# Order of VectorE's instructions in the down projection of a retention, attention and FFN block

## The reference

```python
h = rmsnorm(x, mix_norm_g); z = h @ w_in
x = x + concat([retention(...), mla(...)]) @ w_o
h = rmsnorm(x, ffn_norm_g)
x = x + (silu(h @ w_ffn_gate) * (h @ w_ffn_up)) @ w_ffn_down     # D_FF = 2816
gate = sigmoid(rmsnorm(x, ple_norm_g) @ w_ple_gate)
x = x + gate * (p @ w_ple_proj)
return rmsnorm(x, final_norm_g)
```

## Time and profile before

| what | us |
|---|---|
| median of 3 runs | 1279.24 |
| the profiled execution | 1279.47 |
| its span | 1277.7 |
| busy TensorE (matmul) | 1245.1 |
| busy VectorE | 730.6 |
| busy ScalarE | 480.3 |
| busy GpSimd | 495.1 |

### The profile page before, as it was taken

How to read it: one execution, slowest core, us unless ns; L and a number is a source line. 1 busy time by engine, 2 the same in 40 slices (tenths; PEclk the granted TensorE clock), 3 DMA queues, 4 the chain that set the end, 5 groups by cost and what they waited for, 6 DMA issues and landing times.

```text
span 1277.7 us, 16752 instructions
## 1 busy us (share of the span) xinstructions
PE 1245.1 (97%) x6008; PEld 1046.6 (82%) x6008; DVE 730.6 (57%) x1194; ACT 480.3 (38%) x875; POOL 495.1 (39%) x510
## 2 busy tenths in 40 slices
PE   9999999989998999999999999999999999999997
PEld 8888888877888888878888888888888878788886
DVE  4734444476566226854445454444489999964433
ACT  6622222246565114533333333333344343414421
POOL 2534444440000002364335554334399887610001
PEclk9999999989999999999999999999999999999999
DMA  9411111010012400144233323223454545330002
GB/s 344 147 38 34 50 34 33 1 42 1 0 66 73 143 1 1 38 120 124 85 85 119 120 87 124 93 81 115 156 184 161 191 169 178 115 116 1 1 34 99
DMA packets 101932, 115.10 MB, mean 90 GB/s; under 512 B 4832, under 2 KB 67680, under 8 KB 101856
## 3 DMA queue, kind: packets, MB, share of 16 engines
q1 hardware_dynamic: 101424, 113.57, 27.2%
q10 hardware_dynamic: 432, 0.54, 0.1%
HBM read 90.49 MB, written 23.59 MB: 89 GB/s over the span
## 4 chain that ended last, share of the span: by engine, by line
PE 85%; issue 5%; DVE 4%; POOL 2%; DMA 2%; ACT 2%; SPq 0%; POOLq 0%; ACTq 0%; DVEq 0%
PE PS L1644 10%; PE PS L1642 10%; PE PS L1643 10%; PE PS L206 6%; PE PS L208 6%; PE PS L207 6%; PE PS L1976 4%; PE PS L1977 4%; PE PS L1978 4%; PE PS L994 3%; PE PS L1010 3%; PE PS L2328 2%; PE PS L2330 2%; PE PS L2329 2%; PE PS L789 2%
## 5 line engine op out<-in xcount | busy, mean ns | idle before, releaser
L206 PE MATMUL PS<-WF,HTH 128*128 128x512 f32 (+1 forms) x448 | 177.1, 395 | 1.6 <-DVE WF L184 0.9
L208 PE MATMUL PS<-WF,HTL 128*128 128x512 f32 (+1 forms) x448 | 173.9, 388 | 0.0
L207 PE MATMUL PS<-WF,HTH 128*128 128x512 f32 (+1 forms) x448 | 173.7, 388 | 0.0
L1363 DVE TENSOR_TENSOR X<-X,PS 128x512 f32<-128x512 f32 x172 | 109.9, 677 | 67.4 <-PE PS L208 52.6
L1642 PE MATMUL PS<-HTH,WF 128*128 128x512 f32 x336 | 131.0, 390 | 0.0
L1643 PE MATMUL PS<-HTL,WF 128*128 128x512 f32 x336 | 130.8, 389 | 0.0
L1644 PE MATMUL PS<-HTH,WF 128*128 128x512 f32 x336 | 130.7, 389 | 0.0
L1575 DVE TENSOR_TENSOR WF<-RAW,WF 128x512 fp32r<-128x512 f32 x63 | 69.6, 1106 | 82.4 <-ACT WF L1565 82.4
L1642 PE MATMUL PS<-WF 128*128 128x512 f32 x252 | 98.6, 391 | 2.9 <-issue 2.9
L206 PEld LDWEIGHTS PS<-WF,HTH 128*128 128x128 f32 x448 | 84.7, 189 | 17.5 <-DVE WF L184 1.3
L1644 PE MATMUL PS<-WF 128*128 128x512 f32 x252 | 98.7, 392 | 0.0
(11 more groups left out here) (254 smaller groups left out, 2804.2 us busy)
## 6 DMA issues: line engine op xcount, KB each, us to landing
hid<-TMP SPq DMA_DIRECT2D x74, 256.0 KB, 2.3
TMP<-hid SPq DMA_DIRECT2D x25, 512.0 KB, 5.0
RAW<-in_w_ffn_gate SPq DMA_DIRECT2D x22, 512.0 KB, 4.2
RAW<-in_w_ffn_up SPq DMA_DIRECT2D x22, 512.0 KB, 5.4
RAW<-in_w_ffn_down SPq DMA_DIRECT2D x22, 512.0 KB, 4.1
X<-in_x SPq DMA_DIRECT2D x16, 512.0 KB, 5.3
RAW<-in_w_in SPq DMA_DIRECT2D x32, 256.0 KB, 3.9
TAB<-hid SPq DMA_DIRECT2D x9, 512.0 KB, 4.7
```

The lines of the kernel that those rows point to most:

```text
L206: nc.tensor.matmul(dst, HTH[:, k, tok], w_h, start=(k == 0), stop=False)
L207: nc.tensor.matmul(dst, HTH[:, k, tok], w_l, start=False, stop=False)
L208: last = nc.tensor.matmul(dst, HTL[:, k, tok], w_h, start=False, stop=(k == K - 1))
L1363: nc.vector.tensor_tensor(x, x, src, ALU.add).then_inc(done, 1)
```

## The change

In each step of Down, VectorE's split of a moving operand is issued ahead of all four additions to X instead of between the second and the third. This holds for `ring_lo` (steps 0 to 31) and for the `down_lo` of steps 32 and 33. Pieces, the two last `down_lo` and the streams of all other engines are unchanged.

```diff
             for s in range(STEPS):
-                add_step(e, s, 0)
-                add_step(e, s, 1)
                 if s + 3 < STEPS:
                     ring_lo(e, s + 3)
                 elif s < STEPS - 1:
                     down_lo(e, LAST_ORDER[s + 3 - STEPS])
+                add_step(e, s, 0)
+                add_step(e, s, 1)
                 add_step(e, s, 2)
                 add_step(e, s, 3)
                 if s >= 18 and s % 4 == 2 and s <= 30:
                     piece_lo(e, (s - 10) // 4)
```

## The result

The changed kernel takes 1290.3 us in the median of 6 runs (1287.15 to 1292.87), the kernel before 1278.36 (6 runs, 1275.46 to 1279.64). The ratio is 1.0095, 95% interval 1.0077 to 1.0114: slower by about 12 us. The forecast was 1288.7.

The account below looks back on a forecast made before the run. It took Down to be bound by VectorE and GpSimd, nearly full and taking turns. 1279.24 us plus 2.3 + 5.0 + 4.0 - 4.8 + 3.0 = +9.5 gave 1288.7, own range 1286.5 to 1291, wider 1284.5 to 1291.5.

Parts of the forecast that it names:

- What bounds the stage: In Down, VectorE and GpSimd are nearly full and take turns, each waiting for the other's whole instruction; 4.8 us of waiting.
- Step 2, 2.3 us: TensorE starts step 2 of Down 2.3 us later, waiting for an addition behind a split; bounds 0 to 2.5.
- put off to steps 6 to 9: If no wait came at step 2 of Down, the same 2.3 us would come at steps 6, 7 or 9.
- Step 20, 5.0 us: Step 20 of Down waits 5.0 us for an addition behind a piece (two L184 instructions) and a split; 3.1 to 5.4.
- Step 28, 4.0 us: Step 28 of Down waits 4.0 us for an addition behind a piece and a split; 3.1 to 5.4.
- The 4.8 that go: The 4.8 us of waits in Down before the change are replaced by the new ones: -4.8.
- The clock, 3.0 us: TensorE's clock falls in Down behind the waits at steps 20 (1.3) and 28 (1.7), not step 2: +3.0, bounds 0 to 5.
- The sum: Waits and clock in Down add up to +9.5 us, so the median becomes 1288.7.
- VectorE's busy time: VectorE's busy time in Down, 189.0 of 196 us before, stays about as before.

Follow-up runs that it names:

- Experiment 5: Changed kernel with GpSimd's 35 splits of the stationary operands replaced by memsets that read nothing; 1274.00 us, 0.9969 of the kernel before.
- experiment 1: Kernel before with the new order in steps 0 and 1 alone; 1280.58 us, 1.0016 of the kernel before.
- experiment 4: Changed kernel with 10 and 12 matmuls whose result nothing reads, run in the waits ahead of steps 20 and 28; 1286.54 us, 1.0061 of the kernel before.
- experiment 8: Changed kernel with the pieces after steps 17, 22, 27 and 30 in place of 18, 22, 26 and 30; 1279.81 us, 1.0017 of the kernel before.
- experiment 3: Kernel before with the new order in all steps but 0, 1, 19 and 27; 1277.72 us, 0.9989 of the kernel before.
- experiment 2: Kernel before with the new order in steps 19 and 27 alone; 1285.65 us, 1.0052 of the kernel before.

## Why the prediction was right, and where it was off

- **What bounds the stage.** Right: VectorE and GpSimd taking turns. Experiment 5 takes away the turns with GpSimd's 35 splits, though not those with its sums, and every wait over 0.1 goes with them.
- **Step 2, 2.3 us.** Measured 2.28, and 2.3 in experiments 1, 4 and 8. The remark that it would otherwise be put off to steps 6 to 9 did not come true in experiment 3, which takes the wait away by the old order in steps 0 and 1.
- **Step 20, 5.0 us.** Measured 3.6, but 4.8 and 4.7 in experiments 2 and 4. The term hangs on how long the piece waits for its first turn. I took 2.1 there. With the clock's fall at step 2 TensorE, and with it the last addition of step 18, came 1.7 later against GpSimd's row of instructions; the piece asked at 1041.97 and got its turn 0.8 later, at 1042.75. That GpSimd's row stays put while TensorE slips is what the term assumed, and it held: counted from the kernel before (3.45 added for the earlier start of Down), step 20 starts at 1053.64, and the prediction had 1053.4.
- **Step 28, 4.0 us.** Measured 3.75; 4.1 and 3.7 in experiments 2 and 4. In these two terms half a piece was put at 0.55; alone it takes 0.67 from start to start (experiment 5), too little to matter.
- **The 4.8 that go.** Right: none of the small waits at third products is left.
- **The clock, 3.0 us.** The mis-sized term: 6.3 measured. I had taken no fall at step 2 (there was one, 1.7), 1.3 at step 20 (1.7) and 1.7 at step 28 (2.9, since the clock stayed down for 6.8 us and not 3.4). The 1.3 came from one row, where the fall began 4.1 us after the last matmul ended; here it began 3.2, 3.7 and 2.7 after, so at step 20 none of the slow stretch lay in the wait and at step 28 0.9 of it did. That the falls cost on top of the waits and are not hidden by VectorE was right (experiment 4). The rule of the Trainium skill (TensorE: Matmul & The Clock Gate, "Why this matters for your kernels") that idle gaps send the clock down was the better guide for the two long waits than the stage's own rows of 1.00: both cost the clock, and so did the other waits of 3.2 us or more in Down and near 550 in the ten profiles. For step 2 it decides nothing, since the same wait was followed by a fall here and by none in experiments 1, 4 and 8.
- **The sum.** In the stage +9.5 was forecast and +11.1 measured: 4.85 by waits (6.5 forecast) and 6.3 by the clock (3.0). The two errors have opposite signs and belong together in part, since the fall at step 2 is what shortened the wait at step 20. So it is partly luck that the forecast time lies within 2 us of the measured one. The medians agree with the stage: the mean granted clock over the whole span was 0.9895 in the median of the changed kernel's six executions and 0.994 to 0.995 in the executions of the kernel before that ran beside the experiments. By an estimate from these, 0.0045 to 0.0055 of 1278, the clock takes 6 to 7 us more, and with the 4.85 of the waits that is 11 to 12.
- **VectorE's busy time.** It fell from 189 to 175 us, where I had expected no change: with TensorE late, VectorE stands 27.7 us before additions (5.0 before), and more of its splits find GpSimd idle (9 of 29 run at 1.2 us with no GpSimd instruction beside them between 945 and 1115, before 5 of 30).

```profile
L1363 DVE TENSOR_TENSOR X<-X,PS 128x512 f32<-128x512 f32 x139 | 90.2, 679 | 27.7 <-PE PS L1978 27.5
```

## What to carry to other kernels

When instructions of two engines take turns, as VectorE's splits and GpSimd's do here, look at each run of instructions that takes part and count one of the partner's instructions for each: three of them in a row cost 7.4 us here for 2.5 of work. Put instructions that don't take part, and whose result is wanted next, ahead of such a run, and put such runs where the following results are wanted last; moving two pieces by one step each was worth 3.3 us. Every unfilled wait of 3.2 us or more in Down and near 550 was paid again in clock here, a wait of 2.3 once in four; matmuls whose result nobody reads kept the clock up in the one kernel that ran them.

## What the runs showed of the hardware

- The same wait of 2.3 us at step 2 lowered the clock in one of four profiled kernels (the change; not experiments 1, 4 and 8), so a wait of this size is a draw. Waits of 3.5 us and more in Down, without a fill, lowered it every time: five of five (the change twice, experiment 2 twice, experiment 8 once). The wait ahead of L1642, near 550 in every profile, fits: idle for 1.7 and 2.1 us it was followed by no fall, for 2.6 to 2.9 in three of four, for 3.2 to 3.8 in four of four.
- No size of a wait is safe by these traces. None of Down's waits of 1.8 us and less was followed by a fall, but elsewhere in the kernel falls came behind 1.9 us near 62 and behind 1.6 us near 264 (shorter gaps stand beside that one), in five of the ten profiles each.
- In the ten profiles the clock fell 31 times between 40 and 1200 us; the lower level lasted for 3.4 us in 26 of these and for 6.8 in five. In those five it had begun 0.9 to 1.7 us before TensorE started again (step 28 here and in experiment 2, near 551 in experiments 2, 4 and 5); in the others at most 0.5 before, or after. The length of the wait does not sort them: after 4.8 us at step 20 in experiment 2 it lasted 3.4.
- An addition with one operand in PSUM took 0.67 to 0.69 us beside a busy or an idle GpSimd alike; a split of two SBUF operands took 1.22 alone or beside a memset, and up to 3.4 beside GpSimd's splits and sums.
